# Scattering token numbers by expert and rank during the mix, gathering them per block in the experts, and 96 expert blocks in place of 98

## What is computed

```python
gl = (hf @ router_grp_w) + router_grp_b;  g = argmax(gl)
top_l, top_j = lax.top_k(el_g, 2)                 # two experts of the chosen group
expert = g[:, None] * 8 + top_j
counts = bincount(flat_e, length=32)
padded = (counts + 127) // 128 * 128              # each expert's tokens in blocks of 128
pad_end = cumsum(padded); pad_start = pad_end - padded
dest = pad_start[e_sorted] + arange(m) - start[e_sorted]
slot_tok = full(n_slots, n_tok).at[dest].set(flat_t[order])
blk_e = minimum(searchsorted(pad_end, arange(n_blocks) * 128, side='right'), 31)
xs = h_pad[slot_tok].reshape(n_blocks, 128, d)
yb = (silu(xb @ exp_w_gate[e]) * (xb @ exp_w_up[e])) @ exp_w_down[e]   # per block
```

## Time and profile before

| | |
|---|---|
| median of 3 runs | 8702.04 us (8701.05 to 8733.92) |
| profiled execution | 8742.96 us |
| its span | 8740.9 us |
| busy share of the span | PE 72%, DVE 51%, ACT 46%, POOL 13% |
| DMA | 759 MB, of them 432 MB by POOL's indirect DMAs |

### The profile page before, as it was taken

The page is one execution under the profiler, slowest core; times in us unless marked ns, Lnnn a source line. Parts: engine busy times, 40 slices in busy tenths (PEclk is TensorE's granted clock), DMA queues, the critical chain, the costliest instruction groups (busy, mean ns, idle before and its releaser), DMA issues. The chain is left out here.

```text
span 8740.9 us, 113394 instructions
## 1 busy us (share of the span) xinstructions
PE 6299.1 (72%) x38714; PEld 4220.8 (48%) x38714; DVE 4451.0 (51%) x10781; ACT 4004.5 (46%) x7822; POOL 1098.2 (13%) x1571
## 2 busy tenths in 40 slices
PE   6999965877777777777787761632299939999950
PEld 2777742554544444444555441520155527667640
DVE  1222236777777777777777639346255521001025
ACT  0222224777877787777787740123233302112223
POOL 1222200000000000000000000022011143333334
PEclk8999987999999999999999985666688869999985
DMA  5222210000000000000000001225332228888877
GB/s 184 60 60 60 58 47 5 10 6 11 8 11 9 11 11 11 11 9 8 11 10 8 6 15 51 97 70 58 68 96 96 89 88 328 314 315 330 320 273 243
DMA packets 329209, 759.17 MB, mean 87 GB/s; under 512 B 123533, under 2 KB 187021, under 8 KB 285768
## 3 DMA queue, kind: packets, MB, share of 16 engines
q0 software_dynamic: 71520, 432.08, 13.3%
q1 hardware_dynamic: 257236, 321.70, 12.8%
q10 hardware_dynamic: 54, 0.30, 0.0%
HBM read 589.37 MB, written 162.62 MB: 86 GB/s over the span
## 5 line engine op out<-in xcount | busy, mean ns | idle before, releaser
L953 PE MATMUL at_pC<-at_mark,at_identb 128*128 128x256 bf16 (+1 forms) x5708 | 776.7, 287 | 652.0 <-DVE at_mark L1086 571.4
L953 PEld LDWEIGHTS at_pC<-at_mark,at_identb 128*128 128x128 bf16 x5708 | 538.8, 102 | 868.9 <-DVE at_mark L1086 703.6
L829 ACT ACTIVATE at_relu<-at_pD 128x512 f32<-128x512 f32 (+3 forms) x1136 | 587.1, 563 | 608.6 <-PE at_pD L899 584.6
L1008 DVE CUSTOM_DVE_ANT_0 at_sm<-at_pS,at_drop 128x512 f32<-128x512 f32 (+3 forms) x1152 | 695.7, 641 | 253.8 <-PE at_pS L909 250.9
L1000 DVE SCALAR_TENSOR_TENSOR at_score<-at_relu,keep_IW,at_score 128x512 f32<-128x512 f32 (+3 forms) x994 | 661.7, 707 | 276.8 <-ACT at_relu L829 268.2
L909 PE MATMUL at_pS<-keep_KT,at_q 64*128 64x512 f32 (+3 forms) x2304 | 643.2, 636 | 217.3 <-DVE at_mx L1008 216.9
L844 ACT ACTIVATE at_sm<-at_sm,at_negm 128x512 f32<-128x512 f32 (+3 forms) x1152 | 779.4, 686 | 0.0
L930 PEld LDWEIGHTS at_pO<-at_pt_sb,keep_V 128*64 128x64 f32 x8448 | 468.3, 141 | 420.8 <-issue 374.1
L899 PE MATMUL at_pD<-keep_IKT,at_iq_stack 128*128 128x512 bf16 (+3 forms) x2272 | 588.2, 383 | 65.7 <-DMA at_iq_stack<-scratch_iq_parts 48.9
L919 PE MATMUL at_pT<-keep_ident,at_sm 128*128 128x128 f32 x4224 | 570.5, 277 | 71.5 <-ACT at_sm L844 57.7
L930 PE MATMUL at_pO<-at_pt_sb,keep_V 128*64 128x128 f32 x8448 | 610.7, 287 | 7.9 <-ACT at_oT L872 7.7
(11 more groups left out here) (418 smaller groups left out, 10894.2 us busy)
## 6 DMA issues: line engine op xcount, KB each, us to landing
scratch_ys<-ex_y SPq DMA_DIRECT2D x98, 512.0 KB, 2.7
ada_w_sb<-in_ada_w SPq DMA_DIRECT2D x12, 2048.0 KB, 7.9
scratch_x<-mx_x SPq DMA_DIRECT2D x33, 512.0 KB, 6.6
scratch_h<-mx_h SPq DMA_DIRECT2D x33, 512.0 KB, 2.7
cb_x<-scratch_x SPq DMA_DIRECT2D x33, 512.0 KB, 4.1
pj_x<-in_x_prompt SPq DMA_DIRECT2D x32, 512.0 KB, 3.5
mx_x<-in_x_prompt SPq DMA_DIRECT2D x32, 512.0 KB, 5.9
out_y_prompt<-cb_out SPq DMA_DIRECT2D x32, 512.0 KB, 2.9
```

Of the source, the lines that this page charges most:

```text
L829: e.activation(r[:, n % 4, 0:b - a], pD[:, n % 2, 0:b - a], ACT.Relu).then_inc(s["relu"], 1)
L953: last = e.matmul(pC[:, side, 0:b - a], identb[:, :], mark[:, a:b], start=a == at.start, stop=not constant and b == at.stop)
L1008: last = e.tensor_tensor_reduce(sm[:, u % RING, kv, 0:x.width], pS[:, kv, 0:x.width], drop[:, o:o + x.width], -HD ** -0.5, -NEG, ALU.add, ...
```

## The change

The table of token numbers is laid out by expert and rank instead of by slot: by_rank has room for 4224 tokens (CAP) per expert. Since a token's expert and rank are known in the mix, the scatter moves there: in each step DVE makes slot = expert x CAP + rank for tile st-3, and POOL issues two scatters of that tile's numbers behind its second and third norm chain. The table is cleared by one DMA on SP at the start of the mix. The 96 padding rows of the last tile are no longer counted as tokens (`real`); their numbers go to spare rows (`trash`). The dispatch no longer touches the table; it works out, for every block, the block's expert, its first rank and from both the row of by_rank at which the block begins (now in TOK). In the experts POOL copies that column into ri and gathers the 128 token numbers of block st+3 into ti, one block ahead of the gather of x. NB falls from 98 to 96.

```diff
-NB = -(-(2 * NTOK + NE * (P - 1)) // P)
+NB = (2 * (SEQ + SR) + NE * (P - 1)) // P
+CAP = NTOK
+SPARE = NE * CAP + NB * P
...
 phase_mix, SP
-                e.wait_ge(s["zeroed"], 1)
+                e.wait_ge(s["zeroed"], 6)
+                e.dma_start(S["by_rank"].rearrange("(p b) o -> p (b o)", p=P), empty[:, :]).then_inc(s["cleared"], 16)
                 load_mods(e, S, s["mods"], pr, sa, (2, 4, 3))
...
 phase_mix, POOL, end of a step
+                    t = st - 3
+                    if valid(t):
+                        q = 1 - par
+                        e.wait_ge(s["placed"], t + 1)
+                        for k in range(2):
+                            e.sem_inc(s["taken"], 1)
+                            e.indirect_dma_start(out=S["by_rank"], out_offset=bass.IndirectOffsetOnAxis(ap=slot_i[:, q, k:k + 1], axis=0),
+                                                 in_=tok_q[:, q:q + 1], in_offset=None).then_inc(s[f"scattered{q}"], 16)
                 steps(e, body, ch.restart)
+                e.wait_ge(s["scattered0"], 32 * (T // 2 + 1))
+                e.wait_ge(s["scattered1"], 32 * (T // 2))
...
 phase_mix, DVE, ranks of tile st-3
                             ch.link(e.tensor_copy(meta(2 + k), k1[:, 12 + k:13 + k]))
+                            ch.link(e.scalar_tensor_tensor(slot[:, q, k:k + 1], meta(k), float(CAP), k1[:, 12 + k:13 + k], ALU.mult, ALU.add))
+                            if isinstance(t, int) and t == PT:
+                                ch.link(e.scalar_tensor_tensor(slot[:, q, k:k + 1], slot[:, q, k:k + 1], real[:, :], trash[:, k:k + 1], ALU.mult, ALU.add))
+                        if not isinstance(t, int) or t >= 2:
+                            pair(e, "scattered", t - 2, q, 2)
+                        ch.link(e.tensor_copy(tok_q[:, q:q + 1], tok[:, t:t + 1] if isinstance(t, int) else tok[:, ds(t, 1)]))
+                        e.tensor_copy(slot_i[:, q, :], slot[:, q, :]).then_inc(s["placed"], 1)
+                        e.wait_ge(s["placed"], t + 1)
...
 phase_dispatch, SP and POOL
-                e.dma_start(S["slot_tok"].rearrange("(p b) o -> p (b o)", p=P), zero[:, :]).then_inc(s["cleared"], 16)
-                e.wait_ge(s["scattered"], 16 * 2 * T)
-                e.dma_start(TOK[:, :], S["slot_tok"].rearrange("(b p) o -> p (b o)", p=P), allow_slow_non_contiguous=True).then_inc(s["loaded"], 16)
-                e.wait_ge(s["loaded"], 16)
...
-                for t in range(T):
-                    for k in range(2):
-                        e.indirect_dma_start(out=S["slot_tok"], out_offset=bass.IndirectOffsetOnAxis(ap=DEST[:, k, t:t + 1], axis=0),
-                                             in_=tok[:, t:t + 1], in_offset=None).then_inc(s["scattered"], 16)
...
 phase_dispatch, DVE (the block part now stands ahead of the destinations)
+                e.wait_ge(s["setup"], 16)
...
+                ch.link(e.tensor_tensor(cmp_[:, :, :], slots[:, :].unsqueeze(2).to_broadcast([P, NB, NE]), end[:, :].unsqueeze(1).to_broadcast([P, NB, NE]), ALU.is_ge))
+                ch.link(e.tensor_reduce(be[:, :], cmp_[:, :, :], AX.X, ALU.add))
+                ch.then(e.tensor_scalar(be[:, :], be[:, :], float(NE - 1), None, ALU.min))
+                ch.link(e.tensor_tensor(cmp_[:, :, :], cmp_[:, :, :], pad[:, :].unsqueeze(1).to_broadcast([P, NB, NE]), ALU.mult))
+                ch.link(e.tensor_reduce(first[:, :], cmp_[:, :, :], AX.X, ALU.add))
+                ch.then(e.tensor_scalar(WIDX[:, :], be[:, :], float(P), part[:, :], ALU.mult, ALU.add))
+                ch.link(e.tensor_tensor(first[:, :], slots[:, :], first[:, :], ALU.subtract))
+                ch.link(e.scalar_tensor_tensor(first[:, :], be[:, :], float(CAP), first[:, :], ALU.mult, ALU.add))
+                ch.then(e.tensor_scalar(TOK[:, :], first[:, :], part[:, :], None, ALU.add))
...
 phase_experts, POOL (steps now begin at -3)
+                    b = st + 3
+                    if valid(b):
+                        q = 1 - par
+                        if not isinstance(b, int) or b >= 2:
+                            pair(e, "x", b - 2, q, 1)
+                        e.tensor_copy(ri[:, q:q + 1], column(TOK, b)).then_inc(s["ir"], 1)
+                        e.wait_ge(s["ir"], b + 1)
+                        e.sem_inc(s["tick"], 1)
+                        e.indirect_dma_start(out=ti[:, q:q + 1], out_offset=None, in_=S["by_rank"],
+                                             in_offset=bass.IndirectOffsetOnAxis(ap=ri[:, q:q + 1], axis=0)).then_inc(s[f"t{q}"], 16)
                     b = st + 2
                     if valid(b):
-                        if not isinstance(b, int) or b >= 2:
-                            pair(e, "x", b - 2, par, 1)
-                        e.tensor_copy(ti[:, par:par + 1], column(TOK, b)).then_inc(s["ix0"], 1)
-                        e.wait_ge(s["ix0"], b + 1)
+                        pair(e, "t", b, par, 1)
                         wait(e, s["T"], b - 1)
```

More of the change, by code:

```diff
@@ L1402, in phase_mix @@
         lg = sb("mx_lg", [P, NG + NE]); k1 = sb("mx_k1", [P, 16]); g4 = sb("mx_g4", [P, 2, NG]); el = sb("mx_el", [P, NG, EG]); e8 = sb("mx_e8", [P, 4, EG])
+        real = sb("mx_real", [P, 1]); trash = sb("mx_trash", [P, 2]); slot = sb("mx_slot", [P, 2, 2]); slot_i = sb("mx_slot_i", [P, 2, 2], I32); tok = sb("mx_tok", [P, T], I32); tok_q = sb("mx_tok_q", [P, 2], I32); empty = sb("mx_empty", [P, (SPARE + 2 * P) // P], I32)
         eg = sb("mx_eg", [P, NG]); E = sb("mx_E", [P, 2, 3, NG, EG]); R = sb("mx_R", [P, NE]); junk = sb("mx_junk", [P, NE])
@@ L1407, in phase_mix @@
         names = ("setup mods zeroed wready wown ld0 ld1 sqa sqr ssb rsa rsb rsx Ta aT aa ab ua u ug x1 sqx xn hmul h2 Th hT lg gmax gsum d12 ex choice rk ranked "
-                 "st0 st1 own pool_own tick").split()
+                 "st0 st1 own pool_own tick placed taken cleared scattered0 scattered1").split()
         s = {n: ctx.enter_context(phase_semaphore(nc, "mx_" + n)) for n in names}
@@ L1487, in _ @@
                 e.memset(BASE[:, :], 0.0).then_inc(s["zeroed"], 1)
-                e.wait_ge(s["zeroed"], 5)
+                e.memset(empty[:, :], 0).then_inc(s["zeroed"], 1)
+                e.wait_ge(s["zeroed"], 6)
+                e.iota(tok[:, :], pattern=[[P, T]], base=0, channel_multiplier=1).then_inc(s["zeroed"], 1)
                 e.affine_select(out=lower[:, :], in_=lower[:, :], compare_op=ALU.is_gt, fill=0.0, base=0,
@@ L1570, in _ @@
                 e.wait_ge(s["wready"], DC)
-                e.wait_ge(s["zeroed"], 8)
+                e.wait_ge(s["zeroed"], 10)
                 def body(st, par):
@@ L1628, in _ @@
                 e.wait_ge(s["setup"], 16 * 7)
-                e.wait_ge(s["zeroed"], 8)
+                e.wait_ge(s["zeroed"], 10)
+                ch.link(e.tensor_copy(trash[:, 0:1], tok[:, 0:1]))
+                ch.link(e.tensor_scalar(real[:, :], trash[:, 0:1], float(SR), None, ALU.is_lt))
+                ch.link(e.tensor_scalar(trash[:, 1:2], trash[:, 0:1], float(SPARE + P), None, ALU.add))
+                ch.link(e.tensor_scalar(trash[:, 0:1], trash[:, 0:1], float(SPARE), None, ALU.add))
+                ch.link(e.scalar_tensor_tensor(trash[:, :], real[:, :].to_broadcast([P, 2]), 1.0, trash[:, :], ALU.is_lt, ALU.mult))
                 ch.link(e.tensor_copy(IOTA[:, :], S["IOTAI"][:, :]))
@@ L2007, in phase_dispatch @@
         slots = sb("dp_slots", [P, NB]); cmp_ = sb("dp_cmp", [P, NB, NE]); be = sb("dp_be", [P, NB]); part = sb("dp_part", [P, 1]); pi = sb("dp_pi", [P, 1], I32)
-        tok = sb("dp_tok", [P, T], I32); zero = sb("dp_zero", [P, NB], I32)
-        names = "setup zeroed tokens cleared dest scattered own loaded".split()
+        first = sb("dp_first", [P, NB])
+        names = "setup tokens own".split()
         s = {n: ctx.enter_context(phase_semaphore(nc, "dp_" + n)) for n in names}
@@ L2044, in _ @@
                 ch.link(e.tensor_tensor(start[:, :], end[:, :], pad[:, :], ALU.subtract))
+                e.wait_ge(s["setup"], 16)
+                e.wait_ge(s["tokens"], 1)
+                ch.then(e.tensor_copy(part[:, :], pi[:, :]))
+                ch.link(e.tensor_tensor(cmp_[:, :, :], slots[:, :].unsqueeze(2).to_broadcast([P, NB, NE]), end[:, :].unsqueeze(1).to_broadcast([P, NB, NE]), ALU.is_ge))
[7 more added lines that the diff above has]
+                ch.then(e.tensor_scalar(TOK[:, :], first[:, :], part[:, :], None, ALU.add))
                 for k in range(2):
@@ L2050, in _ @@
                     ch.link(e.tensor_tensor(dest[:, k, :], dest[:, k, :], META[:, :, 2 + k:3 + k].rearrange("p t o -> p (t o)"), ALU.add))
-                e.tensor_copy(DEST[:, :, :], dest[:, :, :]).then_inc(s["dest"], 1)
-                e.wait_ge(s["setup"], 16)
-                e.wait_ge(s["tokens"], 2)
-                ch.link(e.tensor_tensor(cmp_[:, :, :], slots[:, :].unsqueeze(2).to_broadcast([P, NB, NE]), end[:, :].unsqueeze(1).to_broadcast([P, NB, NE]), ALU.is_ge))
```

(7 more changed lines are left out.)

15 lines of the change are left out of this document (6 added, 9 removed).

## The result

| | before | after |
|---|---|---|
| median of 20 runs each, taken together | 8713.77 us | 8752.74 us |
| profiled execution | 8742.96 us | 8753.96 us |
| its span | 8740.9 us | 8752.3 us |

The ratio is 1.0039, with an interval of 1.0026 to 1.0052: the change makes the kernel about 39 us slower, less than 0.5%. I had predicted 8646 us, and a range that ends at 8735. The sum of -56 us was set against the 8702 us of three runs; the median of all 20 lies 12 us higher, so that 12 us of the miss are the base and some 95 us the sum.

A forecast was written before the change was run, and what follows sets the result against it. Bounds: the exposed dispatch chain, and the experts' two-block circle from issuing wd to the gate product. Terms -86, -26, +14, +2, +8, +5, +27 sum to -56 us against 8702.04: 8646 us, range 8603 to 8735.

The forecast's parts named there:

- dispatch: Dispatch stage: scatters and table read-back go, a VectorE chain stays; 28.4 us against 114.05, -86 us.
- two blocks: Experts: two blocks fewer at 13.0 us each, -26 us.
- mix, each step: Mix loop: slots and two scatters move h2 by 4.5 us, partly covered by TensorE waits; +14 us (4 to 33).
- mix, end: End of mix: last tiles' VectorE work, scatters and their landing stand ahead of the stage barrier; +8 us (5 to 11).
- experts, filling: Start of experts: first weights go out 8.5 us later but land about 3 us sooner; +5 us (3 to 8).
- experts, each block: Experts loop: the added gather sends x, wg and wu 1.27 us later behind wd; +27 us (0 to 112).
- The shift is mostly swallowed by the backlog: Experts: queueing ahead of x, wg and wu absorbs most of the 1.27 us, leaving 0.2 us a circle, 10 us.
- ten more circles go over: Experts: ten more two-block turns, wd to gate product, get a slow product behind a longer TensorE wait; 17 us.
- the 5.4 us: Experts: landing time on an empty queue for transfers twice x's size, from x's 4.2 us plus 1.2; used for wg and wu.
- no cover: Experts: all 48 circles grow by the whole 1.27 us with slow products; 112 in place of 27, 8731 us; chance 0.2.
- TensorE at the low clock: Experts: longer waits put more of the following product at 1.2 GHz; 174 in place of 27, 8793 us; chance 0.12.
- Scatters held up in the mix: Mix: all 66 scatters take 3.42 us, h2 4.9 us later in each of 33 steps; +162, 8808 us; chance 0.03.

The follow-up runs named there:

- the last experiment: Kernel before, with GpSimd's last act of the mix a memset behind an added last VectorE operation, no scatter in the mix; 8697.11 us, one run.

## Why the prediction was wrong

| term | predicted, us | profile, us |
|---|---|---|
| dispatch | -86 | -86.9 |
| two blocks | -26 | -26 (taken at the old 13.0) |
| mix, each step | +14 | +0.2 |
| mix, start | +2 | +0.9 |
| mix, end | +8 | +21.3 |
| experts, filling | +5 | +6.9 |
| experts, each block | +27 | +100.3 |
| sum | -56 | +16.7 |

(The steps of the experts: 97 took 1258.2 us before, 95 took 1332.5 after; 74.3 and the two blocks' 26 are 100.3.)

**The step that failed** is the one on each block of the experts: "The shift is mostly swallowed by the backlog", with 0.2 us a circle and "ten more circles go over". wu came 1.2 us later, and 26 more gate products went slow. The error began with the 5.4 us for a transfer twice as large as x on an empty queue: it was worked out from x and a slope, and the trace of the kernel before had rows against it, the first wg and wu of the stage (issued at 7156.75 and 7158.02, with only the first two x ahead of them):

```profile
ex_wg<-in_exp_w_gate,ex_wi POOLq DMA_INDIRECT x1, 8.2
ex_wu<-in_exp_w_up,ex_wi POOLq DMA_INDIRECT x1, 9.5
```

The 5.4 was used for wu too, although wg stands 1.27 us ahead of it; by the prediction's own 2.4 us per MB wu could not have landed before 13.0 us behind wd, where it had 11.9. In the profile after, in the 41 turns that wait, x lands in 4.6 us (median; 6.5 in such turns before), so its queueing did go, but wg still needs 6.8 (7.5) and wu 8.1 (8.8). Of the three microseconds of reserve wu had 0.6. The bounds held, 0 to 112; I took the value near the wrong end, from medians over turns of two kinds. The rival *no cover* priced it at 112 and 8731 us, and it is what happened, by its mechanism nearly in full: the mean circle grew by 0.95 of the 1.2 us, with 44 slow products of the 48 that it supposed. *TensorE at the low clock* happened in part: it would have needed products of some 6.7 us throughout; 13 of the 44 took over 6 us, most of the others 5.4.

What I had not seen is that the cost is a switch. The profile before had it in view: 19 waits of over 2 us, each followed by a turn without one, are 38 of 92 turns that already alternate. The unchanged loop of the last experiment has a step of 12.77 us where the profile before has 13.01, and 98 x 0.24 = 24 us is about half of the 46 us between those two executions.

**Mix, each step.** h2 did move, by 4.1 to 4.3 us behind the ranks in the loop (4.5 predicted), and the shorter step did grow by the 0.9 us that I had derived (21.53 to 22.43). But the longer step shrank by 0.9 (22.89 to 21.98): the pair of steps has a time of its own, and I had charged one half of it.

**Mix, end.** VectorE's last operation came 6.1 us later behind the last join than before (2.6 predicted), the scatters added 3.0 (2.2), and the gap behind them is 12.2 us longer (3). The last is the mis-sized term: the last scatter landed 7.1 us after its issue, so 6.1 us after GpSimd was through with it, and another 12.7 us passed until the dispatch began, where 6.6 was the whole hand-over before.

**Scatters held up in the mix** did not occur: all 66 took 0.95 to 1.10 us, the first of them 0.97 us behind VectorE's slots, as derived. The contention that the Trainium skill tells of (GPSIMD Engine Reference, Specifications) shows in none of them; in the loop VectorE stood still while they were issued.

**Dispatch** came out by its own steps, 27.2 us in place of 28.4. **Filling** came near by luck in part: the first weights left 7.9 us later (8.5 predicted), and wu then landed 1.0 us sooner, not 3; that is the 5.4 us again.

## What to carry to other kernels

When a queue holds a waiting instruction, ask what stands behind it that could go now: here issuing one gather a block later in program order took 139 us off the kernel before (8713.8 to 8575.1), and made the added DMA free. A loop paced by such a circle does not answer to a delay in proportion; if its waits already come in two kinds, price an addition at the full change of kind, not at its length. And a step time that alternates must be costed as a pair.

## What the runs showed of the hardware

- In the changed kernel all gate products but one that had waited over 2 us took 5.1 to 6.8 us in place of 3.7, and 0.43 us of delay on GpSimd were enough to bring 27 more of such slow products (from 18 to 45), 120 us in all (8830.0 against 8709.6 beside it).
- A DMA of 128 pieces of 4 bytes between four large ones did not lengthen the step, once its issue was out of their way: 13.01 us with it in the queue, 13.01 without, and 11.46 in both kernels with wd moved.
- The next stage began 15.8 to 18.8 us behind GpSimd's last instruction where that was an indirect DMA, and 6.6 us where it was a memset (one run).
